# Router logits from turned x1 with scaled router weights, one constant row, and narrow attention scores in alternate banks

## What is computed

```python
x = x + gt1 * token_mixers(h, ...)
h = modulate(rmsnorm(x, g_ffn), sh2, sc2)      # rmsnorm(x)*g_ffn*(1+sc2) + sh2
x = x + gt2 * hier_moe(h, ...)
# in hier_moe
g_logits = xt @ w_group + b_group               # 4 groups
e_logits = xt @ w_router + b_router             # 32 experts
grp = argmax(g_logits); top 2 experts inside the group; weights by softmax
y[token] += weight * (silu(x @ w_gate[e]) * (x @ w_up[e])) @ w_down[e]
```

## Time and profile before

| | us |
|---|---|
| median of 3 runs | 1652.07 (1651.61 to 1652.73) |
| the profiled execution | 1651.5 |
| its span | 1649.6 |
| PE busy | 1532.6 |
| DVE busy | 846.3 |
| ACT busy | 508.6 |
| POOL busy | 205.9 |

### The profile page before, as it was taken

The page is one execution under the profiler, slowest core; times in us unless marked ns, Lnnn a source line. Parts: engine busy times, 40 slices in busy tenths (PEclk is TensorE's granted clock), DMA queues, the critical chain, the costliest instruction groups (busy, mean ns, idle before and its releaser), DMA issues.

```text
span 1649.6 us, 23994 instructions
## 1 busy us (share of the span) xinstructions
PE 1532.6 (93%) x8440; PEld 935.4 (57%) x8441; DVE 846.3 (51%) x1981; ACT 508.6 (31%) x1044; POOL 205.9 (12%) x372
## 2 busy tenths in 40 slices
PE   6999999999999999998999993899999999999992
PEld 3565578789889666666887871333333333333330
DVE  6786887997887677776666545111111111111113
ACT  4326711122212677777222221111111111111113
POOL 0110000000000121000000001122222222222221
PEclk9999999999999999999999995999999999999996
DMA  9650223332211000202576239999899459998995
GB/s 367 217 175 3 88 82 133 96 116 52 52 44 34 27 27 1 78 1 83 177 238 226 85 111 383 369 401 342 311 379 413 119 182 341 403 403 335 414 394 211
DMA packets 122233, 326.32 MB, mean 198 GB/s; under 512 B 14814, under 2 KB 64006, under 8 KB 97570
## 3 DMA queue, kind: packets, MB, share of 16 engines
q1 hardware_dynamic: 110404, 308.36, 49.6%
q0 software_dynamic: 11744, 16.82, 4.5%
HBM read 301.74 MB, written 34.39 MB: 204 GB/s over the span
## 4 chain that ended last, share of the span: by engine, by line
PE 85%; DVE 6%; DMA 4%; issue 2%; ACT 2%; SPq 1%; POOL 0%; POOLq 0%; ACTq 0%; DVEq 0%
PE ps L1487 21%; PE ps L1213 11%; PE ps L1215 11%; PE ps L1214 11%; PE ps L1505 10%; PE ps L1342 4%; PE ps L1355 3%; PE ps L1167 3%; PE ps L1367 3%; DVE arena L1806 2%; DMA arena<-in_w_e_up_dram 2%; DMA arena<-in_w_mod_dram 2%; PE ps L1200 1%; PE ps L1481 1%; PE ps L1170 1%
## 5 line engine op out<-in xcount | busy, mean ns | idle before, releaser
L1487 PE MATMUL ps<-arena 128*64 128x512 f32 x1632 | 374.3, 601 | 13.3 <-issue 9.4
L1487 PEld LDWEIGHTS ps<-arena 128*64 128x64 f32 x1632 | 114.2, 138 | 226.8 <-issue 215.5
L2118 DVE TENSOR_TENSOR arena<-arena,ps 128x256 f32<-128x256 f32 x51 | 21.5, 421 | 403.2 <-ACT arena L1083 403.2
L1505 PE MATMUL ps<-arena 128*64 128x512 f32 x816 | 183.8, 592 | 0.6 <-DVE arena L2134 0.6
L1751 DVE TENSOR_SCALAR_CACHE_REDUCE arena<-arena,small 128x384 bf16<-128x384 f32 (+2 forms) x192 | 169.6, 941 | 0.0
L1213 PE MATMUL ps<-rounded_quad,rounded_pair 128*128 128x512 f32 x352 | 138.5, 393 | 1.3 <-ACT arena L895 1.3
L1215 PE MATMUL ps<-rounded_quad,rounded_pair 128*128 128x512 f32 x352 | 137.1, 390 | 0.0
L1214 PE MATMUL ps<-rounded_quad,rounded_pair 128*128 128x512 f32 x352 | 137.1, 390 | 0.0
L808 POOL DMA_INDIRECT sum_rows<-arena,ones x51 | 81.4, 1597 | 403.1 <-DVE arena L2134 393.9
L1806 DVE CUSTOM_DVE_ANT_0 arena<-ps,arena 128x896 f32<-128x896 f32 (+7 forms) x128 | 91.8, 755 | 70.2 <-PE ps L1342 69.6
L1505 PEld LDWEIGHTS ps<-arena 128*64 128x64 f32 x816 | 58.8, 137 | 116.5 <-issue 116.5
(11 more groups left out here) (314 smaller groups left out, 2421.6 us busy)
## 6 DMA issues: line engine op xcount, KB each, us to landing
arena<-in_w_e_up_dram SPq DMA_DIRECT2D x64, 1024.0 KB, 17.1
arena<-in_w_e_gate_dram SPq DMA_DIRECT2D x64, 1024.0 KB, 14.5
arena<-in_w_e_down_dram SPq DMA_DIRECT2D x32, 2048.0 KB, 14.2
arena<-in_w_mod_dram SPq DMA_DIRECT2D x12, 2048.0 KB, 9.6
plain_pair<-in_w_in_dram SPq DMA_DIRECT2D x30, 512.0 KB, 5.2
arena<-in_x_dram SPq DMA_DIRECT2D x16, 512.0 KB, 7.5
gate_rows<-arena SPq DMA_DIRECT2D x16, 512.0 KB, 3.6
arena<-gate_rows SPq DMA_DIRECT2D x32, 256.0 KB, 3.4
```

Source lines behind the costliest of these rows:

```text
L1487: m = pe.matmul(ps[o * TB:(o + 1) * TB, 2, 0:2 * FQ].rearrange("p (j n) -> p j n", j=2), xT[:, k % NX, k // NX * TB:(k // NX + 1) * TB], w ...
L1505: m = pe.matmul(ps[o * TB:(o + 1) * TB, 5, 0:DQ], hidT[:, k % NH_T, k // NH_T * TB:(k // NH_T + 1) * TB], w_dn[c][:, k, o * DQ:(o + 1) * D ...
```

## The change

The change has four parts.

1. `SCORE_SET` gives narrow units (b below 4) that follow a narrow unit alternately the second bank of each head, and PE then waits only for the unit before the last.
2. The router's weights are scaled by the channel: wgr becomes wgr*(1 + sc2)*g_ffn, and the row sh2 @ wgr + bias is made once, by a reduce on DVE and one matmul with `ones`. The three vectors are loaded as columns. The logits of a block are then rstd * (x1 @ wgr) + row. PE turns x1 instead of h2.
3. On DVE, h2 is made as x1*a2 ahead of the wait for the mean of squares, then *rstd + sh2 in one instruction; the last row block's second step is done on POOL in two instructions for each half. ACT does Square and Sqrt of the last block after the copies of its turned rows.
4. SP and POOL wait in addition for the counts that the new readers of x1 give.

The diff, with names as in the kernel:

```diff
+SCORE_SET = [0]
+for _n in range(1, N_U):
+    SCORE_SET.append(1 - SCORE_SET[-1] if max(UNITS[_n][2], UNITS[_n - 1][2]) < 4 else 0)
...
-        bgr = ones[:, 0:NG + NE]
+        bgr = small[:, late + TT * (NG + NE):late + (TT + 1) * (NG + NE)]
+        spent = wi.rearrange("p t h -> p (t h)")
+        sums_r = spent[:, 0:NG + NE]
+        cols_m = spent[:, NG + NE:NG + NE + 3 * KT].rearrange("p (r k) -> p r k", r=3)
...
             sp.dma_start(gffn, g_ffn[0:1, :].to_broadcast([P, D])).then_inc(mod_out, 16)
+            for j, row in enumerate((mod_d[1:2, :], mod_d[2:3, :], g_ffn[0:1, :])):
+                sp.dma_start(cols_m[:, j, :], row.rearrange("o (t p) -> p (o t)", p=P), allow_slow_non_contiguous=True).then_inc(mod_out, 16)
...
             sp.wait_ge(ssq_ok, 2 * TT)
+            sp.wait_ge(h2t_ps, 2 * TT)
+            sp.wait_ge(ms_ok, 2 * TT)
             weights_dn(0, 0)
...
+            pool.wait_ge(lg_ok, TT + 1)
+            rows = h2[(TT - 1) % 2]
+            for h in (slice(0, 512), slice(512, 1024)):
+                chain.up(pool.tensor_scalar(rows[:, h], rows[:, h], rstd[:, TT - 1:TT], None, ALU.mult))
+            for k, h in enumerate((slice(0, 512), slice(512, 1024))):
+                pool.wait_ge(pool_chain, chain.now() - 1 + k)
+                pool.tensor_tensor(rows[:, h], rows[:, h], sh2[:, h], ALU.add).then_inc(h2_ok, 1)
             pool.wait_ge(yab_ps, N_G)
             pool.wait_ge(x1_ok, 2 * TT)
+            pool.wait_ge(h2t_ps, 2 * TT)
...
+            def squares(t):
...
             for t in range(TT + 1):
...
+                if t < TT - 1:
+                    squares(t)
                 if t >= 1:
                     u = t - 1
                     for h in range(2):
                         act.wait_ge(h2t_ps, 2 * u + h + 1)
                         if u >= 2:
-                            act.wait_ge(lg_ps, u - 1)
+                            act.wait_ge(lg_ps, u)
                         act.activation(h2T[u % 2][h], ps[:, 4 + h, :], ACT.Copy).then_inc(h2t_ok, 1)
+            squares(TT - 1)
...
-                pe.wait_ge(lg_done, 2 * n)
+                pe.wait_ge(lg_done, 2 * n - 2 if n and SCORE_SET[n] != SCORE_SET[n - 1] and b < 4 and UNITS[n - 1][2] < 4 else 2 * n)
...
-                        m = pe.matmul(ps[:, 2 * z + a // 512, 0:e - a], q[half, b * P:(b + 1) * P], k[half, a:e], start=True, stop=True)
+                        m = pe.matmul(ps[:, 2 * z + a // 512 + SCORE_SET[n], 0:e - a], q[half, b * P:(b + 1) * P], k[half, a:e], start=True, stop=True)
...
             def h2_turned(u):
                 for h in range(2):
-                    pe.wait_ge(h2_ok, 2 * u + h + 1)
+                    pe.wait_ge(x1_ok, 2 * u + h + 1)
...
-                        m = pe.transpose(ps[:, 4 + h, j * P:(j + 1) * P], h2[u % 2][:, kt * P:(kt + 1) * P], ident[:])
+                        m = pe.transpose(ps[:, 4 + h, j * P:(j + 1) * P], x1[u][:, kt * P:(kt + 1) * P], ident[:])
...
             def router_logits(u):
-                if u == 0:
-                    pe.wait_ge(r_in, 64)
-                if u >= 2:
-                    pe.wait_ge(lg_ok, u - 1)
+                pe.wait_ge(lg_ok, max(3, u + 2) if u else 2)
...
             for t in range(TT + 2):
+                if t == 2:
+                    pe.wait_ge(lg_ok, 1)
+                    pe.matmul(ps[:, 7, 0:NG + NE], ones[:], sums_r, start=True, stop=True).then_inc(lg_ps, 1)
...
             def modulate_a2():
-                dve.wait_ge(mod_out, 96)
+                dve.wait_ge(mod_out, 144)
...
             def route_in(u):
-                dve.wait_ge(lg_ps, u + 1)
-                dve.tensor_tensor(lgt[:, u, :], ps[:, 6 + u % 2, 0:NG + NE], bgr, ALU.add).then_inc(lg_ok, 1)
+                dve.wait_ge(lg_ps, u + 2)
+                if u == 0:
+                    dve.wait_ge(lg_ok, 3)
+                dve.scalar_tensor_tensor(lgt[:, u, :], ps[:, 6 + u % 2, 0:NG + NE], rstd[:, u:u + 1], bgr, ALU.mult, ALU.add).then_inc(lg_ok, 1)
+            def router_scaled():
+                dve.wait_ge(r_in, 64)
+                router_t = lgt.rearrange("p t e -> p (t e)")[:, 0:KT * (NG + NE)].rearrange("p (t e) -> p t e", t=KT)
+                shift, scale, gain = (cols_m[:, j, :] for j in range(3))
+                chain.up(dve.tensor_tensor(router_t, wgr, shift.unsqueeze(2).to_broadcast([P, KT, NG + NE]), ALU.mult))
+                link(dve.scalar_tensor_tensor(scale, scale, 1.0, gain, ALU.add, ALU.mult))
+                dve.tensor_reduce(sums_r, router_t.rearrange("p t e -> p e t"), AX.X, ALU.add).then_inc(lg_ok, 1)
+                dve.wait_ge(dve_chain, chain.now())
+                dve.tensor_tensor(wgr, wgr, scale.unsqueeze(2).to_broadcast([P, KT, NG + NE]), ALU.mult).then_inc(lg_ok, 1)
+            def router_shifted():
+                dve.wait_ge(lg_ps, 1)
+                dve.tensor_tensor(bgr, bgr, ps[:, 7, 0:NG + NE], ALU.add).then_inc(lg_ok, 1)
...
+                if t >= 2:
+                    dve.wait_ge(h2_out[t % 2], 16 * (t // 2))
+                halves = (slice(0, 512), slice(512, 1024))
+                for k, h in enumerate(halves):
+                    dve.wait_ge(x1_ok, 2 * t + k + 1)
+                    chain.up(dve.tensor_tensor(h2[t % 2][:, h], x1[t][:, h], a2[:, h], ALU.mult))
                 dve.wait_ge(ssq_ok, TT + t + 1)
...
+                for h in halves if t < TT - 1 else ():
+                    dve.scalar_tensor_tensor(h2[t % 2][:, h], h2[t % 2][:, h], rstd[:, t:t + 1], sh2[:, h], ALU.mult, ALU.add).then_inc(h2_ok, 1)
+                if t == 0:
+                    router_scaled()
+                elif t == 1:
+                    router_shifted()
+                else:
                     route_in(t - 2)
             route_in(TT - 2)
             route_in(TT - 1)
...
             dve.wait_ge(dc_ok, 1)
-            dve.wait_ge(lg_ok, TT)
+            dve.wait_ge(lg_ok, TT + 3)
```

More of the change, by code:

```diff
@@ L1046, in _ @@
             high_m(3)
+            def squares(t):
+                act.wait_ge(x1_ok, 2 * t + 2)
+                if t >= 1:
+                    act.wait_ge(ssq_ok, TT + t)
+                act.activation(sqj, x1[t], ACT.Square, accum_out=ssq[:, t:t + 1]).then_inc(ssq_ok, 1)
+                act.wait_ge(ms_ok, TT + t + 1)
+                act.activation(rstd[:, t:t + 1], ssq[:, t:t + 1], ACT.Sqrt).then_inc(sqrt_ok, 1)
             for t in range(TT + 1):
@@ L1051, in _ @@
                     high_m(t + 2)
-                if t < TT:
-                    act.wait_ge(x1_ok, 2 * t + 2)
-                    if t >= 1:
-                        act.wait_ge(ssq_ok, TT + t)
-                    act.activation(sqj, x1[t], ACT.Square, accum_out=ssq[:, t:t + 1]).then_inc(ssq_ok, 1)
-                    act.wait_ge(ms_ok, TT + t + 1)
-                    act.activation(rstd[:, t:t + 1], ssq[:, t:t + 1], ACT.Sqrt).then_inc(sqrt_ok, 1)
+                if t < TT - 1:
+                    squares(t)
                 if t >= 1:
@@ L1805, in largest @@
                         added = sc[:, MOFF[b]:MOFF[b] + w]
-                    dve.tensor_tensor_reduce(lg[n % 4][z][:, 0:w], ps[:, 2 * z:2 * z + 2, :].rearrange("p a n -> p (a n)")[:, 0:w],
+                    dve.tensor_tensor_reduce(lg[n % 4][z][:, 0:w], ps[:, 2 * z + SCORE_SET[n]:2 * z + 2, :].rearrange("p a n -> p (a n)")[:, 0:w],
                                              added, -1.0 if kind == "b" else -root, 3e38, ALU.add, ALU.min,
@@ L1987, in _ @@
                 link(dve.reciprocal(rstd[:, t:t + 1], rstd[:, t:t + 1]))
-                if t >= 2:
-                    dve.wait_ge(h2_out[t % 2], 16 * (t // 2))
-                    dve.wait_ge(h2t_ps, 2 * (t - 1))
-                halves = (slice(0, 512), slice(512, 1024))
-                for h in halves:
-                    chain.up(dve.scalar_tensor_tensor(h2[t % 2][:, h], x1[t][:, h], rstd[:, t:t + 1], a2[:, h], ALU.mult, ALU.mult))
-                for k, h in enumerate(halves):
-                    dve.wait_ge(dve_chain, chain.now() - 1 + k)
-                    dve.tensor_tensor(h2[t % 2][:, h], h2[t % 2][:, h], sh2[:, h], ALU.add).then_inc(h2_ok, 1)
-                if t >= 2:
+                for h in halves if t < TT - 1 else ():
[5 more added lines that the diff above has]
+                else:
                     route_in(t - 2)
```

## The result

The changed kernel takes 1658.85 us (median of 9 runs, 1656.95 to 1662.88), the kernel before on the same chip 1652.40 (9 runs). The ratio is 1.0033, 95% interval 1.0022 to 1.0045: slower by 3.6 to 7.4 us, 5.5 as the middle. I had forecast +3.6. The direction was right and the size too small; the median is 0.05 us above the upper end of the range, the ratio times the median shown before, 1657.5, is inside it.

A forecast was written before the change was run, and what follows sets the result against it. The prediction took DVE's routing start, with PE idle behind it, to bound the kernel; 3.55 us there and 0 for the rest gave +3.6 us, 1652.07 to 1655.7 us, with an 8-in-10 range of 1652.3 to 1658.8.

The forecast's parts named there:

- What bounds the kernel: PE's gap from 984 to 1009 us: DVE's routing start, 987.80 before, moves the kernel's end one for one.
- Part 1: Attention scores in alternate banks: worth 0, bounds 0 and -6.8 us, since narrow units start without idle time.
- Part 2: Column loads and scaled router weights: loads 0, DVE's operations hidden, one extra matmul +0.2 us.
- Part 3: Last row block: block 5's reading delays logits and Pool, so DVE starts the routing 3.55 us later.
- Pool's four operations: Pool's last row block arithmetic ahead of its constants: 1.0 us each, 4.0 together, bounds 2.2 and 7.0.
- Pool is quick: Rival at the last row block: Pool's four operations take under 3.75 us, +1.8 to +3.2, 1654.6; chance 0.26.
- the sum: Whole kernel: 3.55 us at the routing start, extra matmul included, and 0 for the rest: +3.6 us.
- Part 4: SP's last h2 store and expert weights 6.5 us later: cost 0, caught up at 1040 to 1060; bounds -1, +3.
- late weights bite: Rival behind the routing: the later weight stream delays the gather or an early expert, 3 us on top, 1658.7; chance 0.08.
- given back: Rival at the gather: it lands some 3 us sooner, 1652.5; chance 0.12 together with no effect.

The follow-up runs named there:

- e5: e1 with ACT's Square and Sqrt of the last row block moved ahead of its copies; 1652.59 us, ratio 1.0002 to the kernel before.
- e4: The kernel before with only the alternate score banks (SCORE_SET) added; 1653.49 us, ratio 1.0008.
- e1: The changed kernel with the last row block's second step on DVE instead of Pool; 1656.2 us, ratio 1.0015 to the kernel before.
- c1: The changed kernel run again without an edit, as reference for the others; 1660.0 us, ratio 1.0040 to the kernel before.
- e6: The kernel before with SP's remaining expert weights held until the routing's second semaphore; 1655.9 us, ratio 1.0021.
- e9: e5 with the last h2 store issued from ACT's queue; 1652.21 us, ratio 0.9995 to the kernel before.
- e10: The changed kernel with the third expert's gate and up loads, and SP's later work, held until the second block's gate and up finish; 1664.39 us.
- e3: The changed kernel with the last h2 store issued from ACT's queue instead of SP's; 1656.81 us, ratio 1.0023 to the kernel before.
- e7: The changed kernel with Pool's multiplication as tensor_tensor with the column broadcast instead of tensor_scalar; 1657.45 us, one run.
- e2: The changed kernel with Pool's constants made first and its last row block arithmetic behind them; 1658.48 us, ratio 1.0042 to the kernel before.

## Why the prediction was right, and where it was too small

**What bounds the kernel.** "Whatever moves the start of the routing moves the end of the kernel one for one" holds for a delay and fails for a gain: e5 started it 2.9 us earlier and won nothing that 12 runs show. Between the routing and the experts' steady stretch there is a second path, SP's stream of weights: where it is still running when PE comes to the second block, that block starts later and runs slower. I had looked at both and taken the second for slack.

**Part 1** at 0: right, by the waits and e4.

**Part 2** at 0 and +0.2: right as far as the trace shows. The operations of `router_scaled`, DVE in the changed kernel:

```profile
898.77 0.46 DVE L2000 TENSOR_TENSOR small<-arena,small 128x288 f32<-128x288 f32 x1
899.13 0.16 DVE L2001 SCALAR_TENSOR_TENSOR small<-small 128x8 f32<-128x8 f32 x1
899.33 0.67 DVE L2002 TENSOR_REDUCE small<-small 128x36 f32<-128x288 f32 x1
899.92 0.45 DVE L2004 TENSOR_TENSOR arena<-arena,small 128x288 f32<-128x288 f32 x1
```

1.6 us where I had allowed 2.3, hidden behind PE's group. The extra matmul cost 0.26 us, as forecast at 0.2. e5, which has parts 1 and 2 whole, is the kernel before within 0.1%; since it also has a gain and a loss that cancel, it is no test of part 2 by itself, and none was made.

**Part 3**: the mechanism is as forecast. What put the last logits off is that `squares(7)` stands behind ACT's copies and `lg_ok` 9 behind both; turned round (e1 to e5) it is worth 2.1 us of the total, though the intervals of the two overlap. The last pass took 2.96 us, between the 3.6 forecast and the 1.95 that it takes at full clock in e5, where PE idled less (2.36 to 3.63 in the other versions with the late reading). The mis-sized term is Pool's four operations: 5.6 us, not 4.0, within the bounds of 2.2 and 7.0. The addition took 1.24 us, the multiplication by a column 1.57; the select, which I took as nearest, stood too low. The Trainium skill, "GPSIMD Engine Reference", section "3.1 Elementwise — side-by-side cycle accounting", is near on the first by its rate for tensor_tensor (a quarter of its 4497 ns for 2048 columns, an estimate of 1.1; the prediction has 1.2) and low on the second, where its 769 ns for a simple loop of 512 columns lies under both forms measured here (1.57 and 1.02). Its section "4.1 Engine selection", which sends such work to VectorE, was borne out: DVE did both halves in 1.41 us, and e1 is 4.1 us faster than c1. With more than 3.75 us for the four, the rival "Pool is quick" is out. By this term alone the sum becomes 3.55 + 1.6 = 5.2 us, where the trace has 4.9 with the extra matmul.

**Part 4** at 0 is the step that failed, and the rival "late weights bite" (chance 0.08, 1658.7) was nearer. It reads: "the late stream is caught up there". The slack at 1040 to 1060 exists, but it lies behind the gap. The stream was also timed too short: forecast to end at about 1024, the last of its eleven loads landed at 1033.2 (issued at 1002.98, 30.2 us to landing), and the third expert's down weights, which the sum leaves out, at 1038.2. e6 prices the step by itself, with a stream held 2.4 us longer: +3.5 us (1.8 to 5.1). The rival's mechanism was not mine either: neither the gather nor an expert waits for data. The gather took 7.49 us, as forecast from 7.32, so "given back" is out. What the stream does is lengthen PE's gap between the first two blocks from about 1.9 to about 4.0 us and leave the matmuls behind it at the lower clock for a while, 5.35 to 6.17 us for sixteen instead of 3.65.

**Two costs and one total.** 4.9 at the routing and 3.5 for the stream would be 8.4 us, beyond the upper end of the range; measured are 5.5 and 6.6. Why the medians show less than the sum is not known. The profiled executions of the changed kernel show no saving: against the turn of block 6 they are 8.6 (after) and 8.5 us (c1) behind the kernel before at the third block, and their gaps, 3.92 and 3.82 us, are as long as e6's 4.00. But both are slower than their medians, and the others were not profiled; the executions of one kernel lie up to 12 us apart here (e9). So it is in part luck that a forecast with part 4 at nothing has the right sign and comes this near. That Pool's arithmetic costs 4.1 us (c1 to e1) contains both costs, since the last h2 store and all the weights stood behind it.

## What to carry to other kernels

- A store whose data comes late must not stand in a queue ahead of loads that need nothing from it. Ask of each queue what stands behind the instruction that you put off, and when that stream would have ended, not only when its data is needed.
- A gain on one of two paths that end at nearly the same time can be given back by the other: e5 shortened the routing, and the time stayed. It need not be the only loss: e9 took the second path out at the second block, and the time stayed too. Look for the moment where they meet (here the second expert block) before you price either.
- Work that moves to an engine to relieve another has to be off the path there: the 1.41 us that left DVE came back as 5.6 on Pool, with the routing and the weights behind it.

## What the runs showed of the hardware that I had not expected

- **PE's gap before the second block of experts is short or long with the DMA traffic that PE meets there.** In that gap the program waits for DVE, reads registers and takes branches. The gap was 1.79 us at DMA share 0.04 (e10), 1.87 at 0.14 (before), 1.91 at 0.31 (e9), and 3.92, 4.00 and 4.01 us at 0.76 to 1.01 (after, e6, e5). All twelve profiles fall in two groups: 1.59 to 1.91 us where the first wave had landed or was held back (before, e3, e4, e9, e10), 3.82 to 4.24 us where it had not (the other seven); in c1 the wave landed only 1.7 us after PE came there.
- **Traffic is not all of it.** Before the fourth block the DMA share was 0.99 or more in all twelve gaps, and they lasted 1.81 to 3.22 us: up to 2.08 in the three kernels that have the output projection of before (before, e4, e6), 2.54 and more in the nine others. What makes this difference was not tested; that the code in front is other is one rival.
- **What is slowed in the gap stays open.** The Trainium skill, "Runtime: NRT & Kernel Launch", section "🔬 Instruction fetch mechanics", states that a taken branch whose target isn't near can force a DMA fetch of instructions before the engine goes on, which would explain it. The traces don't settle it and rather speak against: the DMA view has an instruction packet of 0.02 MB inside the gaps of e3 and e10, two of the short ones, but none inside those of the other ten (in the changed kernel, 1036.4 to 1040.4 us, one just before and one just after). Whether the branch or the register reads are slowed is not shown. For e10 from 1031.6 to 1033.6 (queue: packets, MB, share):

```profile
q8 instruction: 1, 0.02, 3.8%
```

- **The clock behind the gap**: after 1.6 to 2.4 us of idle PE the matmuls ran on at full speed, 3.65 us for sixteen; after 3.2 to 4.2 us they took 4.98 to 6.53. In between it went either way: 3.65 after 2.96 us (e5), 4.97 after 2.98 (after). So 2 us more of gap before the second block cost about 4, of which some 1 us came back at the next gap.
- **Pool's multiplication by a column** takes 1.57 us for 128x512 as tensor_scalar and 1.02 as tensor_tensor with the column broadcast (e7).
- **Pool's tensor_tensor holds up DVE's two-input operations** (0.19 us became 1.09 and 1.18 in e2); beside its tensor_scalar one of them kept its 0.19.
